# How each partition's share of two expert weight matrices is laid out: eight far rows of 2 KB, or eight consecutive rows as one run of 16 KB

## The reference

```python
t = rms_norm(h, norm_moe_g).reshape(B * S, D)            # 1024 tokens x 1024 features
# ... gates: top-1 of 4 groups, then top-2 of its 4 experts, softmax weights
moe = jnp.zeros_like(t)
for e in range(N_EXPERTS):                                # 16
    he = jax.nn.silu(t @ w_gate[e]) * (t @ w_up[e])       # 1024 -> 512
    moe = moe + gates[:, e:e + 1] * (he @ w_down[e])      # 512 -> 1024
h = h + moe.reshape(B, S, D)
```

## Time and profile before

| | us |
|---|---|
| median of 3 runs | 1438.11 (1437.15 to 1438.55) |
| the profiled execution | 1440.33 |
| its span | 1438.3 |
| attention and routing, up to the first slot's product | about 1030 |
| nine slots with a tail, a turn each | 24.3 |
| eight turns of the second loop, 1251.0 to 1410.4, together | 159.4 |

### The profile page before, as it was taken

One profiled execution on the slowest core, in us unless ns is written; L12 is line 12 of the kernel. 1 busy time (PEld: TensorE's weight loads), 2 busy tenths in 40 slices (PEclk: granted clock), 3 DMA queues, 4 the chain that ended last, 5 costly groups with the idle time before them and its releaser, 6 DMA issues.

```text
span 1438.3 us, 21798 instructions
## 1 busy us (share of the span) xinstructions
PE 1357.7 (94%) x8048; PEld 1019.1 (71%) x8048; DVE 882.4 (61%) x1686; ACT 777.3 (54%) x1466; POOL 140.0 (10%) x207
## 2 busy tenths in 40 slices
PE   6999999999999999999999999997799999999995
PEld 5888998744445554447887877885578787888784
DVE  5513124557649876776775433347776767688886
ACT  6321376456656766674334334335176766677775
POOL 1000000012220110000000000000131323211111
PEclk9999999999999999999999999998799999999998
DMA  6231114530020000102130010033299989999995
GB/s 234 47 134 45 62 60 171 191 140 1 1 87 31 1 1 30 58 31 88 45 143 4 30 59 31 30 126 138 92 333 285 341 282 337 306 380 368 365 360 208
DMA packets 96742, 203.99 MB, mean 142 GB/s; under 512 B 14439, under 2 KB 25343, under 8 KB 95906
## 3 DMA queue, kind: packets, MB, share of 16 engines
q1 hardware_dynamic: 87346, 182.89, 35.3%
q0 software_dynamic: 7248, 20.20, 5.5%
q10 hardware_dynamic: 2080, 0.01, 0.1%
HBM read 178.95 MB, written 26.35 MB: 143 GB/s over the span
## 4 chain that ended last, share of the span: by engine, by line
PE 76%; DMA 9%; DVE 5%; ACT 5%; issue 3%; POOL 0%; ACTq 0%; DVEq 0%; POOLq 0%; SPq 0%
PE psum L2230 26%; PE psum L2478 18%; DMA up_stage<-in_w_up 8%; PE psum L2214 8%; PE psum L2373 7%; PE psum L2396 5%; PE psum L2355 4%; PE psum L2207 3%; PE psum L2652 2%; DVE up_rest L1783 2%; PE psum L2659 1%; ACT up_high L1301 1%; ACT arena L1466 1%; ACT arena L1276 1%; PE psum L2640 1%
## 5 line engine op out<-in xcount | busy, mean ns | idle before, releaser
L970 ACT ACTIVATE arena<-psum 128x512 f32<-128x512 f32 (+3 forms) x195 | 85.7, 494 | 84.1 <-PE psum L2396 46.4
L2373 PE MATMUL psum<-arena 64*128 64x512 f32 (+7 forms) x384 | 115.6, 520 | 5.8 <-ACT arena L1257 3.6
L1668 DVE TENSOR_TENSOR_SCAN arena<-arena,singles 128x768 f32<-128x768 f32 (+7 forms) x64 | 86.3, 1363 | 53.7 <-POOL arena L828 47.6
L2214 PE MATMUL psum<-arena 128*128 128x512 f32 (+2 forms) x352 | 118.0, 487 | 0.8 <-DVE arena L1649 0.8
L1783 DVE TENSOR_TENSOR up_rest<-up_stage,up_high 128x1024 fp32r<-128x1024 f32 x76 | 89.6, 1220 | 23.1 <-ACT up_high L1301 23.0
L1783 DVE TENSOR_TENSOR down_rest<-down_stage,down_high 128x1024 fp32r<-128x1024 f32 x72 | 85.6, 1220 | 27.9 <-ACT down_high L1301 27.9
L2396 PEld LDWEIGHTS psum<-ident,arena 128*128 128x128 f32 x576 | 65.8, 143 | 52.0 <-ACT arena L970 25.8
L2373 PEld LDWEIGHTS psum<-arena 64*128 64x128 f32 (+1 forms) x384 | 49.2, 190 | 73.2 <-issue 49.4
L2214 PEld LDWEIGHTS psum<-arena 128*128 128x128 f32 x352 | 65.1, 190 | 42.7 <-issue 27.0
L2396 PE MATMUL psum<-ident,arena 128*128 128x128 f32 x576 | 85.3, 285 | 8.5 <-DVE arena L1668 4.4
L2207 PE MATMUL psum<-ident,arena 128*128 128x128 f32 (+1 forms) x520 | 73.4, 278 | 18.9 <-ACT arena L988 9.5
(11 more groups left out here) (481 smaller groups left out, 3387.1 us busy)
## 6 DMA issues: line engine op xcount, KB each, us to landing
gate_stage<-in_w_gate SPq DMA_DIRECT2D x19, 2048.0 KB, 9.1
up_stage<-in_w_up SPq DMA_DIRECT2D x19, 2048.0 KB
down_stage<-in_w_down SPq DMA_DIRECT2D x18, 2048.0 KB, 9.5
arena<-in_x SPq DMA_DIRECT2D x16, 512.0 KB, 3.5
arena<-in_w_mkv SPq DMA_DIRECT2D x8, 1024.0 KB, 6.2
arena<-in_w_in SPq DMA_DIRECT2D x4, 1024.0 KB, 11.1
arena<-in_w_mo SPq DMA_DIRECT2D x4, 1024.0 KB, 6.6
mv_times_w_mo_spill<-arena SPq DMA_DIRECT2D x8, 512.0 KB, 3.2
```

The source lines that it names most:

```text
L970: do(act.activation(dst, src, ACT.Copy), s_te["act"])
L1668: do(dve.tensor_tensor_scan(w_row(u, r, a)[:, 0:L][:, ::-1], f_sb[:, n % FAILS, 0:L][:, ::-1], tiny.to_broadcast([P, L]), 1.0, ALU.mult, A ...
L2214: mm = pe.matmul(dst, a, b, start=(i == 0), stop=(i == n - 1))
L2373: mm = pe.matmul(scores_of(kind, n)[:, at:end], lhs, rhs(at, end), start=True, stop=True)
```

## The change

Two things that belong together.

1. `load` reads gate's and up's matrices so that partition p takes the rows 8p to 8p + 7. They are contiguous in DRAM, and the staging tile's row in a partition is contiguous too: 16 KB in one piece, where before partition p took the rows p, 128 + p, 256 + p, ..., eight pieces of 2 KB. Down's load (rows of 4 KB) stays.
2. `tn` is written in the matching order. Feature 128a + 8q + k goes to column 128k + 16a + q, so that block k after the transposition has feature 8p + k in partition p = 16a + q. DVE's writes now step by 128 floats (512 bytes) from one element to the next; the reads are contiguous as before. This holds for the seven whole tiles (L1862) and the two halves of the last (L2024). The columns of a quarter still are two whole blocks, so the tail's gather is unchanged.

No instruction is added, removed or moved on any engine; every line behind the edits only has a new number (+1 to +4).

```diff
@@ -323,6 +323,7 @@
         tn = mq_sb
+        tn_spread = tn.rearrange("p (k a q) -> p a q k", k=DC, a=DC)
         tT = mqT
@@ -633,7 +634,10 @@
             def load(e, part, cond=None):
 
-                src = (w_gate, w_up, w_down)[part][bass.ds(e, 1), :, :].rearrange("e (k p) n -> p (e k) n", p=P)
+                if part == 2:
+                    src = w_down[bass.ds(e, 1), :, :].rearrange("e (k p) n -> p (e k) n", p=P)
+                else:
+                    src = (w_gate, w_up)[part][bass.ds(e, 1), :, :].rearrange("e (p k) n -> p (e k) n", p=P)
                 sp.dma_start(stage[part][:, :, :], src, cond=cond).then_inc(s_st[part], 16)
@@ -1859,8 +1863,8 @@
-                do(dve.scalar_tensor_tensor(out=tn.rearrange("p (a b) -> p a b", a=DC), in0=h2[:, :, tile_of(j)],
-                                            scalar=rt2[:, 0:1], in1=moe_g.rearrange("p (a b) -> p a b", a=DC),
+                do(dve.scalar_tensor_tensor(out=tn_spread, in0=h2[:, :, tile_of(j)].rearrange("p a (q k) -> p a q k", k=DC),
+                                            scalar=rt2[:, 0:1], in1=moe_g.rearrange("p (a q k) -> p a q k", a=DC, k=DC),
                                             op0=ALU.mult, op1=ALU.mult), s_tn)
@@ -2021,8 +2025,8 @@
-                do(dve.tensor_tensor(tn[:, 512 * half:512 * half + 512].rearrange("p (a b) -> p a b", a=4), h2[:, v, last],
-                                     moe_g[:, 512 * half:512 * half + 512].rearrange("p (a b) -> p a b", a=4), ALU.mult), s_hg)
+                do(dve.tensor_tensor(tn_spread[:, v, :, :], h2[:, v, last].rearrange("p a (q k) -> p a q k", k=DC),
+                                     moe_g.rearrange("p (a q k) -> p a q k", a=DC, k=DC)[:, v, :, :], ALU.mult), s_hg)
```

## The result

The kernel after the change is slower, by little: median 1441.70 us of 18 runs (1438.13 to 1447.45) against 1436.81 us for the kernel before, run beside it. The ratio is 1.0034, 95% interval 1.0025 to 1.0044. The forecast was 1432.2 us, range 1428 to 1440, with a chance of 11% for slower.

What follows compares the result with a forecast made beforehand. The prediction took PE to set the first loop's turns and the DMA engines the second's. Faster loads (-6.5 us) and the strided write (+0.6) made -5.9 us, from 1438.1 to 1432.2 us, range 1428 to 1440.

Steps and rivals of the forecast that it cites:

- The rate: Loads of gate and up: 16 KB pieces would run at 425 to 435 GB/s, saving 0.48 us a load.
- Rival (a): Loads of gate and up: the rate doesn't rise, being held by HBM or a shared DMA path; 1438.7 us, chance 0.14.
- (d): Loads of gate and up: pieces of 16 KB are themselves slow; about 1500 us, chance 0.03.
- three quarters of the saving: Second loop: of 8.6 us of DMA work saved, 6.5 us would become time.
- rival (c): POOL's gathers queue behind long weight pieces, tightest at the first loop's tail gather; 1441.2 us, chance 0.09.
- (b): Second loop: DMA engines go idle as often as they get faster, a third of 8.6 us stays; 1435.8 us, chance 0.13.
- PE's floor: Second loop: PE needs 18.1 us a turn, 144.8 us for eight, so better DMA gives at most 14.6 us.
- The first loop: PE's 24.30 us turn hides the loads there, so nothing was counted and the turn would stay.
- Part 2: DVE's strided write of `tn` in the last tile's routing would cost 0.6 us, bounds 0 and 2 us.
- The sum: Whole kernel: -6.5 us for the loads and +0.6 us for the strided write make -5.9 us.

Runs made afterwards that it cites:

- both loops reordered: In both loops POOL starts the gathers before waiting for the last scatters, added to the changed kernel with 16 KB pieces: ratio 0.9949 to the kernel before, median 1430.68 us.

## Why the prediction was wrong, step by step

**The rate: right, a little large.** 423 GB/s against 425 to 435. At 423 a load costs 4.96 instead of 5.34 us, 0.38 us saved where 0.48 was put; the gain ended at 8 KB (424 GB/s), where a further 1.4% (427 to 433) was put on 16 KB; in the kernel with both loops reordered the same 16 KB loads show 427. 18 x 0.38 is 6.8 us instead of 8.6. Rival (a), no rise, is refuted. The Trainium skill ("DMA: Bandwidth & Descriptors", Specifications) has the line rate from 512 B on; for such loads the measurement decides otherwise, with 393, 415 and 424 GB/s for 2, 4 and 8 KB of the same matrix. (d) is refuted too.

**That three quarters of the saving becomes time: the wrong step.** The term was -6.5 us, and it rested on queue 0's transfers staying as they are ("the other 4.2 are the gather and the accumulating scatter, which don't change"). They did change, in the second loop, for which rival (c) gave the all-clear. The prediction wrote: "The scatter in the second loop has more room: it starts after the copy L1466 ends (about 1308), lands 7.1 us later, 10.4 at most, and is waited for by the next L1466 at 1324.92; 8 x 0.52 = 4.2 us more fits." Two things failed in it. The delay was larger than these 4.2 us: the scatter's median went from 8.7 to 14.5 us in that loop, 5.8 us more, with 16.5 at worst, and the gather behind it from 6.6 to 10.0. (With both loops reordered the scatter takes 12.5 us, 3.8 more: there the price of (c) fits.) And the one that waits for it first isn't ACT's L1466 but POOL itself, which doesn't copy the next slot's indices, and so doesn't start the gather, until the scatter has landed. The trace of before had this wait (17.6 us, two times), and the order of `fetch`, `add_rows` and the wait on s_ya is in the code. So the delays of scatter and gather add up in one chain: from the scatter's start at 1288.07 to the transposes at 1319.58 it is 31.5 us, in a turn of 20.3. Cutting that one link brings the ratio from 1.0034 to 0.9969 in one loop and 0.9949 in both: shown. The mechanism was the one named under (c), priced at a place (the first loop's tail gather) where it doesn't decide. The prediction had also put down as its sign of being wrong that "the rate rises and the turns don't get shorter", and that is what came. A DMA share under 1, its sign for (b), came too; but under (b) the reordering would have brought nothing back.

**PE's floor: misread.** The prediction took the short turn's 18.1 us for PE's floor, 144.8 us for eight turns, so 14.6 us to be gained. But the earlier trace rows have PE busy for 151.01 us in these eight turns, 18.9 a turn; a long turn simply holds more of its work (19.12). At most 8.4 us could be gained, and with both loops reordered 7.8 were (151.6 instead of 159.4).

**The first loop: right.** Turns of 24.30 us, and no wait of PE for the tail gather; its landing rose from a median of 6.4 to 7.2 us. There was room for it, as priced.

**Part 2: right in size, too dear on the chain.** 2091 and about 1090 ns against 2040 and 1070; on the path 0.1 us in the profile instead of 0.6, and nothing that can be measured (1.0035 without it, 1.0034 with it).

**The sum.** -5.9 us was forecast for an order of POOL's work that lets the loads set the turn. The version in which they do has -7.3 us. With POOL's order as it is, the change has +4.9. Of these, the profile pair holds 3.4 us in the second loop; where the rest lies is not shown. The two falls of PE's clock there take away up to those 3.4 us, a term that the prediction did not have. The other runs point the same way: of their traces, the second loop has two such falls without the strided write, one with 8 KB pieces in one transfer and POOL's old order, and none in any other. The granted clock over the whole span is 0.9786 on average in the 18 runs of after and 0.9779 in those without the strided write; in the runs of all other kernels here it is 0.980 to 0.981, those of the kernel before included. An estimate from these means: 0.0024 x 1440 = 3.5 us at full speed. So the late queue costs the kernel the gain and leaves PE idle longer, and most of what it is slower than the kernel before may be the clock that falls behind that. No run holds the clock fixed, so this share isn't shown.

**What stays open.** Why 4 and 8 KB give no time with the old order, although with 4 KB the index copy waits for the scatter in only four or five turns of eight. Why the reordering in the first loop, whose turns are 24.3 us with and without it, adds to the one in the second (0.9969 to 0.9949 with 16 KB, 0.9976 to 0.9939 with 8 KB); the eight turns of the second loop are 2.1 us shorter with it (151.6 against 153.7), and the first index copy there no longer waits 12.0 us for a scatter of the first loop. 8 and 16 KB, both loops reordered, differ by less than their intervals.

## What to carry to other kernels

A change that makes one queue's transfers faster by longer pieces has to be priced on every transfer of the other queues, and that price has to be followed through the issuing engine's own order, not only to the consumer of the data: look for the wait that stands between one small transfer and the next. When a faster resource gives no time and its busy share falls (here from 1.02 to 0.96), name what now starts late, cut that link alone, and run the same cut on the old kernel; the change may be good and only the order wrong. A buffer that is shared by two independent steps, here two columns of one index tile, is such a link. Splitting its use costs one more copy, here 0.7 us in the median on an engine that has time for it. And look at PE's clock wherever a change leaves PE idle: the idle time may not be all that is lost.

## What the runs showed of the hardware

- **Small transfers beside long pieces.** The accumulating scatter of 128 rows of 4 KB landed after 8.7 us (median) beside 2 KB pieces and 14.5 us beside 16 KB pieces. With one transfer for a matrix it was 9.8 us beside 4 KB and 11.1 beside 8 KB, and 12.5 beside 16 KB with both loops reordered. The gather went from 6.6 to 10.0 us in POOL's old order; in the new one it lands after 6.7 us beside the same 16 KB pieces, so its lateness isn't a matter of the pieces alone. The Trainium skill ("DMA: Bandwidth & Descriptors", Queues, rings and completion order) has an engine change queues only after a packet of some 9 to 17 descriptors. The prediction drew from this that "by it the gathers would hardly wait longer than now". That did not follow, since a turn of a fixed number of descriptors gets longer as they do, and the scatter's time does grow with the piece. How many descriptors an engine takes at a time no run here shows.
- **Alternate pieces start slowly.** The first pair of loads with 4 KB pieces that leave out every other one ran at 336 GB/s from 962 to 966 us; the same size with no gaps ran at 416 there. From 966 us on the alternate pieces had 415 too. One execution each, and the cause is open.
- **A write with a step of 512 bytes** costs DVE 2091 ns for 1024 columns instead of 1284, about what the read with this step costs over a contiguous one (754 ns by the earlier trace rows; here 807).
- **POOL's small copy beside DVE.** A copy of 128x2 integers takes 0.18 us. In the kernel after, where the late scatter puts it beside DVE's remainders, it took up to 2.0 us, and 5.8 us in the kernel without the strided write. The spread of the eight copies (ns, min/median/max), of before and of after:

```profile
L894 POOL COPY idx<-idx_all x8: 184/184/185, 1258.3 to 1397.9; 128x2 int32 x8
```

```profile
L898 POOL COPY idx<-idx_all x8: 186/624/2026, 1259.6 to 1403.6; 128x2 int32 x8
```

  The remainder reads two tensors in SBUF. The Trainium skill ("SBUF — State Buffer", SBUF: two separate sides) says that such a DVE instruction and a POOL instruction that reads SBUF exclude each other on one pair of ports for a whole instruction. The trace fits this, and shows more: the copy of 5.82 us, begun at 1403.96, outlasted four such instructions in a row (1403.97 to 1408.59). No run takes DVE's work away beside it, so the cause is read from the timelines alone.
